# Hybrid DSA / RWKV-7 / MLA step: another order in the attention loops, two output tiles begun early, one split moved to POOL

## What is computed

```
for i in range(DEPTH):                      # 4 layers, kind = i % 3
    hn = rmsnorm(x, n_mix[i])
    out = (dsa, rwkv7, mla)[kind](hn, ...)
    x = x + out                             # out = o @ w_out, 1024 x 1024
    x = x + conv_ffn(rmsnorm(x, n_ffn[i]))  # silu(gate) * val, 2816 wide
dsa:  score[t,s] = sum_h wi[t,h] * relu(qi[t,h] . ki[s]);  keep a quarter of the keys per query (64 or 48)
      prob = softmax(where(kept, q . k * scale, -inf));  o = prob @ v
mla:  logits = (q_nope . k_nope + q_pe . k_pe) * scale, softmax, @ v
```

## Time and profile before

| | us |
|---|---|
| runs | 1801.41, 1799.29, 1799.11 (median 1799.29) |
| profiled execution | 1800.91, of which span 1799.1 |
| PE / DVE / ACT / POOL busy | 1678.7 / 1173.9 / 855.7 / 717.5 |
| layer 0: first logits to the third output tile | 93.84 to 161.87 |
| layer 2 (MLA): second projected pair's logits to the third output tile | 1067.44 to 1138.11 |

### The profile page before, as it was taken

The page is one execution under the profiler, slowest core; times in us unless marked ns, Lnnn a source line. Parts: engine busy times, 40 slices in busy tenths (PEclk is TensorE's granted clock), DMA queues, the critical chain, the costliest instruction groups (busy, mean ns, idle before and its releaser), DMA issues.

```text
span 1799.1 us, 37483 instructions
## 1 busy us (share of the span) xinstructions
PE 1678.7 (93%) x14117; PEld 1592.1 (88%) x14117; DVE 1173.9 (65%) x2069; ACT 855.7 (48%) x1600; POOL 717.5 (40%) x801
## 2 busy tenths in 40 slices
PE   7978999996988997999999988999999997999997
PEld 6857999994778997999999877999999885999997
DVE  4775777737477455577755647577764586677743
ACT  3444566433653433465633444465643445556532
POOL 5641566400035110366611354266621760466600
PEclk9998999998999998999999998899999998999999
DMA  7313555454231002455555211355546511555453
GB/s 199 105 34 95 140 153 150 125 150 126 78 110 30 5 9 79 139 142 150 138 145 172 86 50 48 107 151 147 149 129 160 157 49 48 141 140 156 125 146 95
DMA packets 344896, 205.09 MB, mean 114 GB/s; under 512 B 22456, under 2 KB 342184, under 8 KB 344656
## 3 DMA queue, kind: packets, MB, share of 16 engines
q1 hardware_dynamic: 342640, 199.76, 38.8%
q0 software_dynamic: 2144, 3.77, 0.8%
HBM read 200.02 MB, written 3.39 MB: 113 GB/s over the span
## 4 chain that ended last, share of the span: by engine, by line
PE 80%; DVE 11%; ACT 5%; issue 3%; POOL 1%; DMA 0%; SPq 0%; DVEq 0%; ACTq 0%; POOLq 0%
PE bank L877 23%; PE bank L878 23%; PE bank L879 23%; PE bank L1205 4%; DVE lo L1984 2%; PE bank L888 1%; ACT hi L1495 1%; ACT LS L1528 1%; DVE LS L2036 1%; DVE LS L2027 1%; DVE SC L2160 1%; PE bank L938 1%; PE bank L1229 1%; PE bank L1144 1%; POOL lo L666 1%
## 5 line engine op out<-in xcount | busy, mean ns | idle before, releaser
L877 PE MATMUL bank<-XH,hi 128*128 128x320 f32 (+1 forms) x1992 | 630.3, 316 | 15.8 <-DVE lo L1984 7.7
L1984 DVE TENSOR_TENSOR lo<-raw,hi 128x2048 fp32r<-128x2048 f32 (+3 forms) x201 | 428.7, 2133 | 309.5 <-ACT hi L1495 309.5
L878 PE MATMUL bank<-XL,hi 128*128 128x320 f32 (+1 forms) x1992 | 621.4, 312 | 0.0
L879 PE MATMUL bank<-XH,lo 128*128 128x320 f32 (+1 forms) x1992 | 621.4, 312 | 0.0
L877 PEld LDWEIGHTS bank<-XH,hi 128*128 128x128 f32 (+1 forms) x1992 | 377.4, 189 | 30.2 <-DVE lo L1984 10.4
L1495 ACT ACTIVATE hi<-raw 128x2048 fp32r<-128x2048 f32 (+4 forms) x205 | 359.8, 1755 | 74.6 <-PE bank L879 65.1
L878 PEld LDWEIGHTS bank<-XL,hi 128*128 128x128 f32 (+1 forms) x1992 | 377.9, 190 | 1.3 <-issue 0.2
L879 PEld LDWEIGHTS bank<-XH,lo 128*128 128x128 f32 (+1 forms) x1992 | 377.4, 189 | 0.0
L702 POOL TENSOR_TENSOR upad<-upad,rstd 128x128 f32<-128x128 f32 (+1 forms) x176 | 167.7, 973 | 199.8 <-ACT upad L1574 199.8
L877 PE MATMUL bank<-GH,hi 128*128 128x322 f32 x704 | 219.8, 312 | 3.6 <-DVE lo L1984 3.6
L878 PE MATMUL bank<-GL,hi 128*128 128x322 f32 x704 | 218.7, 311 | 0.0
(11 more groups left out here) (379 smaller groups left out, 2436.0 us busy)
## 6 DMA issues: line engine op xcount, KB each, us to landing
raw<-in_f_w_up SPq DMA_DIRECT2D x176, 512.0 KB, 5.0
raw<-in_f_w_down SPq DMA_DIRECT2D x64, 704.0 KB, 4.7
raw<-in_a_w_in SPq DMA_DIRECT2D x12, 1024.0 KB, 5.3
raw<-in_b_w_rkv SPq DMA_DIRECT2D x12, 1024.0 KB, 5.1
raw<-in_a_w_out SPq DMA_DIRECT2D x8, 1024.0 KB, 5.2
raw<-in_b_w_out SPq DMA_DIRECT2D x4, 1024.0 KB, 5.3
raw<-in_c_w_out SPq DMA_DIRECT2D x4, 1024.0 KB, 5.1
raw<-in_a_w_in SPq DMA_DIRECT2D x12, 256.0 KB, 4.8
```

What stands on the lines that cost most here:

```text
L877: pe.matmul(out, a, xh(k), start=(start and k == 0), stop=False)
L878: pe.matmul(out, a, xl(k), start=False, stop=False)
L879: last = pe.matmul(out, b, xh(k), start=False, stop=(stop and k == kt - 1))
L1984: dve.tensor_tensor(lo[n % 2][:, 0:w_], raw[n % 2][:, 0:w_], hi[n % 2][:, 0:w_].bitcast(F32), ALU.subtract).then_inc(w_lo, 1)
```

## The change

In words, by its parts:

1. **Loop order (DSA and MLA).** PE: `pair_qk(p + 2)` stands ahead of `turn_probs(p)`. ACT: `exps(p + 2)` ahead of `out_hi(p)`. DVE: `maxima(p + 2)` ahead of `pt_copy(p)`. In DSA tiles 15 and 16 are projected before the loop, and DVE has `probs(0)` ahead of `maxima(1)`.
2. **Output tiles begun.** After `values` of pair 5 PE makes the blocks k = 0 to 4 of output tile 0, after pair 6 the blocks 0 to 5 of tile 1; `attention_out` makes what is left.
3. **Splits.** In DSA the low part of query slab s0+5 goes from DVE to POOL, behind POOL's stores, and that of the first output slab from DVE to POOL, behind the last rotary turn; ACT makes its high part after pair 2 instead of pair 4. POOL's split of s0+7 is in one piece behind the mask's copy.
4. **Forms.** `probs`: three TENSOR_TENSOR with a broadcast reciprocal in place of five TENSOR_SCALAR. Score of head 0 and the large mask: SCALAR_TENSOR_TENSOR with a broadcast constant in place of TENSOR_SCALAR.
5. **RWKV.** `split_lo(s0 + 10)` before `bonus(0)`, `split_lo(s0 + 11)` after `bonus(1)`; one head sum one tile later on PE.

```diff
+            def out_begun(layer, p):
+                s0, last = first_slab[layer, "out"], Q0[layer] + PAIRS
+                m, end = (0, 5) if p == 5 else (1, 6)
+                pe.wait_ge(max_done, last)
+                pe.wait_ge(ol_done, Q0[layer] + end)
+                ready(s0)
+                product(psum[4 + m][:, 0:T], s0, 128 * m, lambda k: OH[:, k, :], lambda k: OL[:, k, :], end=end)
+            def attention_out(layer):
...
+                            before=(lambda k: pe.wait_ge(ol_done, q + k + 1)) if m == 0 else None, first=(5, 6, 0)[min(m, 2)])
...
@@ PE, DSA @@
                 pair_qk(0)
+                project(15)
                 pair_qk(1)
-                project(15)
+                project(16)
                 for p in range(PAIRS):
-                    turn_probs(Q + p)
                     if p + 2 < PAIRS:
                         pair_qk(p + 2)
+                    turn_probs(Q + p)
...
-                    if p == 0:
-                        project(16)
-                mixer_out(layer, lambda k: OH[:, k, :], lambda k: OL[:, k, :], lambda: pe.wait_ge(ol_done, Q + PAIRS))
+                    if p in (5, 6):
+                        out_begun(layer, p)
+                attention_out(layer)
...
@@ PE, RWKV @@
-                bonus_at = {18: (0,), 19: (1,), 20: (2, 3), 21: (4,), 22: (5, 6), 23: (7,)}
+                bonus_at = {18: (0,), 19: (1,), 20: (2,), 21: (3, 4), 22: (5, 6), 23: (7,)}
...
@@ ACT, DSA @@
                     pt_copy(Q + p)
-                    out_hi(Q + p, p)
                     if p + 2 < PAIRS:
                         exps(Q + p + 2)
-                    if p == 0:
-                        evac(16)
-                    if p == 4:
+                    out_hi(Q + p, p)
+                    if p == 2:
                         split_hi(s0 + 8)
...
@@ DVE, probs @@
-                for u, (a, b) in enumerate(UNITS):
-                    ins = dve.tensor_scalar(LS(q)[:, a:b], LS(q)[:, a:b], rsum[:, slot(q), u:u + 1], None, ALU.mult)
-                ins.then_inc(prob_done, 1)
+                heads = LS(q)[:, 0:768].rearrange("p (e n) -> p e n", e=2)
+                for first, a, b in ((0, 0, 128), (1, 128, 384)):
+                    r_ = rsum[:, slot(q), first:first + 3:2].rearrange("p (e o) -> p e o", o=1).to_broadcast([128, 2, b - a])
+                    dve.tensor_tensor(heads[:, :, a:b], heads[:, :, a:b], r_, ALU.mult)
+                dve.tensor_tensor(LS(q)[:, 768:960], LS(q)[:, 768:960], rsum[:, slot(q), 4:5].to_broadcast([128, 192]), ALU.mult
+                                  ).then_inc(prob_done, 1)
...
@@ DVE, DSA @@
-                split_lo(s0 + 5)
...
+                probs(Q)
                 maxima(Q + 1, masks, A_SCALE)
                 swap(Rb + 12, E + 15, SWAP_A)
-                probs(Q)
                 for p in range(PAIRS):
+                    if p + 2 < PAIRS:
+                        maxima(Q + p + 2, masks, A_SCALE)
                     pt_copy(Q + p)
                     if p + 1 < PAIRS:
                         probs(Q + p + 1)
-                    if p + 2 < PAIRS:
-                        maxima(Q + p + 2, masks, A_SCALE)
...
-                    if p == 5:
-                        dve.wait_ge(w_lo, s0 + 8)
-                        split_lo(s0 + 8)
+                dve.wait_ge(w_lo, s0 + 9)
```

More of the change, by code:

```diff
@@ L831, in _ @@
                         store(dst[2], KIo[0:n_, z, :])
+                    split_lo(first_slab[layer, "mix"] + 5, 0, 4)
                     for p in range(PAIRS):
@@ L867, in parts, with product @@
                 return (t[n % 2][:, 0:s.kt * s.w].rearrange("p (k w) -> p k w", w=s.w) for t in (hi, lo))
-            def product(out, n, c0, xh, xl, m=128, start=True, stop=True, before=None):
+            def product(out, n, c0, xh, xl, m=128, start=True, stop=True, before=None, first=0, end=None):
                 wh, wl = parts(n)
                 kt = slabs[n].kt
-                for k in range(kt):
+                for k in range(first, end or kt):
                     if before:
@@ L879, in product @@
                     last = pe.matmul(out, b, xh(k), start=False, stop=(stop and k == kt - 1))
-                last.then_inc(mm_done, 1)
+                if end is None:
+                    last.then_inc(mm_done, 1)
             def x_ready(j):
@@ L2502, in dve_mla @@
                 for p in range(PAIRS):
+                    if p == 0:
+                        dve.wait_ge(stored, 16 * STORES_AT["latent"])
+                    if p + 2 < PAIRS:
+                        maxima(Q + p + 2, masks, C_SCALE)
                     pt_copy(Q + p)
```

45 lines of the change are left out of this document (27 added, 18 removed).

## The result

The changed kernel takes 1813.24 us (median of 4, 1811.92 to 1816.28) against 1799.54 us: a ratio of 1.0073, 95% interval 1.0057 to 1.0089. It is 13.7 us slower where 6 us faster was forecast, outside the range (1774 to 1805) and on the other side. The profiled execution took 1816.28 us with a span of 1814.5.

The account below looks back on a forecast made before the run. PE was taken as the bound, with gains only where it stands or runs at the lower clock. DSA -7.4 (two layers), RWKV -4.4, MLA +5.4 sum to -6.4 us: 1793 us against 1799.29, 8-in-10 range 1774 to 1805.

Parts of the forecast that it names:

- The score stage: DSA, DVE's score sums beside POOL's split: 3.6 us of waiting plus 1.1 at the low clock, +4.7 us per layer.
- They take turns whole: DVE and POOL operations on SBUF alternate one whole operation at a time; DSA score sums 1.3 to 1.5 us each.
- The pair's cycle in DSA: DSA attention loop: a steady pair takes 4.80 instead of 5.22 us, but the start is longer; +0.1 us per layer.
- has it ready some 5 us before its first use: DSA tail: POOL finishes the first output slab's low part some 5 us before it is first used.
- The tail in DSA: From pair 5's transposes to the third output tile: 20.0 us against 28.55, -8.5 us per layer.
- the tiles begun hide nothing: Rival: first output slab's low part is late, half the tail's gain goes in two layers, +8.5, 1801.5 us; chance 0.07.
- The mask: DSA, large mask on DVE: falls from 3.27 us to about 0.5 plus the wait for one POOL part.
- RWKV: Layer 1: PE's 4.26 us wait for slab s0+10's split goes; -4.4 us, bounds 0 and -6.
- I follow them to 572.4: RWKV: with DVE's later heads 2.3 us behind, the 24 tiles end at 572.4 against 576.8.
- MLA: Layer 2: loop slower by 7.9 us, tail 2.5 us shorter, in all +5.4 us; bounds -3.5 and +18.
- The closed loop: MLA: PE's logits wait for POOL's rotary turns, behind DVE's shuffles, copy and maxima; 9.6 us an iteration.
- MLA decides: Rival: the MLA loop, slower, with the low clock in every iteration; MLA +18, 1805.5 us; chance 0.18.

Follow-up runs that it names:

- the run with the mask first: Changed kernel, but POOL waits for the large mask before it splits query slab s0+7; 1820.31 us, ratio 1.0115 to the kernel before.
- the slab between the multiplications: Changed kernel, but POOL splits the first output slab in two halves, behind pair 4's and pair 5's multiplications; 1809.04 us, ratio 1.0046 to the kernel before.
- the run with gaps: Changed kernel, but POOL waits for each of a split's four parts before starting the next; 1811.26 us, ratio 1.0072 to the kernel before.

## Why the prediction was wrong, step by step

- **The score stage** (+4.7 a layer): the mechanism was right, and the first query tile comes 4.8 and 5.1 us later. The term that was mis-sized is the wait for POOL, 3.6 us; the low clock of the first query tile added 0.8 and 1.5, against 1.1 in the term. "They take turns whole" failed here, though it held for pair 4's multiplications: one sum started ahead of POOL's row and waited for three parts, 4.46 us in one piece, where 1.3 to 1.5 us for each sum were forecast. Why it takes turns in one place and not in the other is open.
- **The pair's cycle in DSA** (4.80 us): measured 4.80. The term of the whole loop (+0.1) was +2.9 and +3.2. The step that failed is in the tail's paragraph, where POOL "has it ready some 5 us before its first use" was taken to mean that the split is free. It is ready in time, but its 5.7 us lie on the multiplications of pair 4. The split in two halves gives 3.3 and 2.9 us back, the whole of it. The prediction had named the multiplications as exposed to POOL, and gave that no price here.
- **The tail in DSA** (-8.5): -8.2 and -8.1 measured, with a wrong reason inside. The sum gave the begun tiles a gain (what is left of the two tiles hides beside the splits behind pair 7). They lose 2 us: the tail without them is 17.9 us. Behind pair 7's values PE has 7 us of its own for tiles 0 and 1, which cover `out_hi` and both parts of the next slab (4.6 us); begun early, their 33 matmuls push pair 7's values, and so those splits, back by 4.3 us, and PE then waits 2.6 us. What the change gained there must be the splits taken out of the last pairs, and the clock; one of them put back on DVE costs 3.0 and 3.5 us of the tail, the others were not tested one by one. The rival "the tiles begun hide nothing" had the effect, but put it down to a late slab.
- **The mask** (0.5 us and one part): 5.14 us, and of no consequence, as the run with the mask first shows. That POOL's turns behind the split set the start was in the prediction. The 0.5 us and one part were no more than the reading "they take turns whole": the mask waited through the rest of one part, two more and two operations of a rotary turn.
- **RWKV** (-4.4): -0.3 at the recurrence. That the wait of 4.26 goes was right. What failed is "I follow them to 572.4": the split of s0+11 had moved too, ahead of the rows of pair 3, whose sum PE wants at 559.76, and it takes 2.96 us there. With it behind those rows the stage is 3.5 us shorter (29.2 us instead of 32.7), and the recurrence starts at 572.10.
- **MLA** (+5.4): +10.2. The closed loop was right, its undisturbed iteration 9.89 against 9.6 (bounds 9.2 to 9.9), and the first split added 1.3 against 1.8. The term that was mis-sized is the low clock: 3.2 us were added once, but in the trace PE's logits, transposes and values are inside the loop, and pair 5's logits come 12.93 us after pair 4's, with no split in the way and no wait for POOL, by PE's own work at 0.60 of the clock. The five iterations take 57.6 us against 51.9 and 3.2. This size depends on the execution: the eight traces with this loop have 53.8 to 57.6, and the forecast 55.1 lies among them. And the tail's gain of 2.5 us is 0 (26.3), from the begun tiles (22.8 without them) and 0.78 of the clock. The rival "MLA decides" had this mechanism at 18 us.
- **Small slips in the sums**, of no weight: the score stage's bounds, 5.8 less 1.2 and less 0.6 to 1.5, are 3.1 to 4.0 and not 3.3 to 4.0, and 3.6 is not their upper end; PE's own work in an MLA iteration adds up to 8.9, and 8.96 was measured.
- **The rest**: 3.7 us of the profiled difference are spread of the unchanged part.

By the medians the miss is 20 us: 9 of it in the two DSA layers, mainly their loops and score stages, 5 in MLA, 4 in RWKV, and about 2 of spread.

## What to carry to other kernels

Before an instruction is moved ahead of another, follow the loop through every engine: here two shuffles behind the maxima instead of ahead of them cost 12 to 18 us, with the same work. Work given to a second engine is not free because it is ready in time; look at what shares its memory port in the same microseconds, and put it where the other engine reads PSUM. And matmuls done early help only if nothing that ends later is queued behind them: the cover that they gave to the last splits was worth more.

## What the runs showed of the hardware

- A DVE operation on SBUF that meets a row of POOL's SBUF operations back to back can wait for several of them. Head 0's sum waited for three parts (4.46 us for an operation of 0.48); the mask waited for five operations, until a gap of 0.08 us between two of a rotary turn (5.14 us for 0.56). With such gaps between POOL's parts, the mask took 1.20 us and head 1's sums waited a part each. TENSOR_SCALAR waited in the same place as the two-input form (6.18 us for three).
- It need not wait so long. In the same trace pair 4's multiplications got in behind one part each, although POOL's parts followed each other without a gap (131.59 to 133.34), and POOL's parts became 1.45 and 1.71 us long instead of 1.27. What decides between the two is open. The Trainium skill, "SBUF — State Buffer", section "Who interferes with whom", calls the shared port pair an exclusive lock. The turns of pair 4 agree with that, and a wait through several instructions of the other engine is not told there.
- How much each side is stretched depends on the form. Beside rotary turns, three TENSOR_TENSOR took 2.9 us and POOL's operations 0.94 to 1.32; five TENSOR_SCALAR took 3.35 us and left POOL's at 0.87 to 1.01.
- DVE's maxima and copies from PSUM were not held by POOL (the slab between the multiplications).
- DVE was also held at times while POOL only issued stores: head 0's first operation 1.43 us (0.35 alone) in layer 3, and the 128x256 one 1.55 us in the run with gaps. Others beside the same stores kept their 0.35 and 0.48 us, and a split on DVE its 2.29. Why is open.
